# Convolution taps ahead of the steps of a block inverse, on VectorE

## The reference, cut to what matters

```python
proj = h @ mix_w_in
qkv = silu(causal_depthwise_conv(concat([q, k, v]), conv_w))      # 4 taps along the tokens
qh = l2_normalize(q) * 128 ** -0.5;  kh = l2_normalize(k);  vh = v
kk = kh @ kh^T in each chunk
a_mat = strict_lower(beta * kk * decay)
sol = triangular_solve(a_mat + I, rhs)                            # unit lower triangular
...                                                               # a scan over the chunks
```

## Time and profile before

| | us |
|---|---|
| median of 3 runs (lowest, highest) | 2188.54 (2186.83, 2190.27) |
| the profiled execution, its own time | 2190.45 |
| its span | 2188.8 |
| PE busy | 2042.5 (93%) |
| DVE busy | 1008.9 (46%) |
| ACT busy | 819.9 (37%) |
| POOL busy | 170.1 (8%) |

### The profile page before, as it was taken

The page is one execution under the profiler, slowest core; times in us unless marked ns, Lnnn a source line. Parts: engine busy times, 40 slices in busy tenths (PEclk is TensorE's granted clock), DMA queues, the critical chain, the costliest instruction groups (busy, mean ns, idle before and its releaser), DMA issues.

```text
span 2188.8 us, 26092 instructions
## 1 busy us (share of the span) xinstructions
PE 2042.5 (93%) x9478; PEld 1661.5 (76%) x9478; DVE 1008.9 (46%) x1464; ACT 819.9 (37%) x1358; POOL 170.1 (8%) x193
## 2 busy tenths in 40 slices
PE   6999876689989999999999998999989999999998
PEld 5888655566668887788888777788868877888886
DVE  6687434444434333533333375955454334333332
ACT  4342331344543233443432265433343324343332
POOL 1102002000000002000001111004300010000010
PEclk9999987589999999999999999999999999999999
DMA  8868305011103333233332322221223432333321
GB/s 286 262 177 289 108 1 118 21 41 35 39 3 99 98 99 87 77 96 96 96 99 87 114 75 71 81 71 42 58 68 89 136 97 77 97 94 102 99 86 59
DMA packets 336376, 209.63 MB, mean 96 GB/s; under 512 B 21225, under 2 KB 323238, under 8 KB 336038
## 3 DMA queue, kind: packets, MB, share of 16 engines
q1 hardware_dynamic: 325072, 170.58, 27.6%
q0 software_dynamic: 10368, 37.75, 4.9%
q10 hardware_dynamic: 854, 0.20, 0.0%
HBM read 203.26 MB, written 5.24 MB: 95 GB/s over the span
## 4 chain that ended last, share of the span: by engine, by line
PE 79%; DVE 10%; ACT 4%; DMA 3%; issue 2%; ACTq 1%; POOL 0%; DVEq 0%; SPq 0%; POOLq 0%
PE psum L425 22%; PE psum L427 21%; PE psum L426 21%; DVE delta_qkv_T L1896 2%; PE psum L1065 2%; DMA ada_w<-in_ada_w 2%; PE psum L1266 1%; PE psum L1084 1%; PE psum L1016 1%; PE psum L967 1%; PE psum L982 1%; DVE w_lo L384 1%; DVE ada_sum L1896 1%; PE psum L1074 1%; PE psum L878 1%
## 5 line engine op out<-in xcount | busy, mean ns | idle before, releaser
L425 PE MATMUL psum<-act_hi,w_hi 128*128 128x512 f32 x1616 | 649.6, 402 | 17.8 <-DVE w_lo L384 7.0
L427 PE MATMUL psum<-act_hi,w_lo 128*128 128x512 f32 x1616 | 637.0, 394 | 0.0
L426 PE MATMUL psum<-act_lo,w_hi 128*128 128x512 f32 x1616 | 636.9, 394 | 0.0
L384 DVE TENSOR_TENSOR w_lo<-w_raw,w_hi 128x1024 fp32r<-128x1024 f32 x306 | 386.1, 1266 | 376.3 <-ACT w_hi L376 354.4
L425 PEld LDWEIGHTS psum<-act_hi,w_hi 128*128 128x128 f32 x1616 | 307.7, 190 | 110.1 <-issue 42.6
L376 ACT ACTIVATE w_hi<-w_raw 128x1024 fp32r<-128x1024 f32 x306 | 319.7, 1052 | 172.2 <-PE psum L427 155.8
L427 PEld LDWEIGHTS psum<-act_hi,w_lo 128*128 128x128 f32 x1616 | 307.6, 190 | 66.5
L426 PEld LDWEIGHTS psum<-act_lo,w_hi 128*128 128x128 f32 x1616 | 308.2, 191 | 61.6 <-issue 0.5
L703 POOL TENSOR_TENSOR squares<-squares 128x512 f32<-128x512 f32 x30 | 46.2, 1549 | 1414.4 <-ACT squares L1453 911.6
L425 PE MATMUL psum<-ffn_hi,w_hi 128*128 128x512 f32 x352 | 139.6, 396 | 0.0
L427 PE MATMUL psum<-ffn_hi,w_lo 128*128 128x512 f32 x352 | 139.0, 395 | 0.0
(11 more groups left out here) (350 smaller groups left out, 2519.3 us busy)
## 6 DMA issues: line engine op xcount, KB each, us to landing
w_raw<-in_ffn_w_in SPq DMA_DIRECT2D x88, 512.0 KB, 3.8
ada_w<-in_ada_w POOLq DMA_DIRECT2D x72, 512.0 KB, 5.7
w_raw<-in_w_in SPq DMA_DIRECT2D x68, 512.0 KB, 3.9
w_raw<-in_mix_w_in SPq DMA_DIRECT2D x52, 512.0 KB, 3.8
w_raw<-in_ffn_w_out SPq DMA_DIRECT2D x32, 512.0 KB, 3.7
w_raw<-in_ffn_w_out SPq DMA_DIRECT2D x16, 384.0 KB, 3.2
w_raw<-in_w_branch_a SPq DMA_DIRECT2D x8, 512.0 KB, 3.6
w_raw<-in_w_out SPq DMA_DIRECT2D x8, 512.0 KB, 3.6
```

What stands on the lines that cost most here:

```text
L384: dve.tensor_tensor(WLO[:, n % 4, :], RAW[:, n % 4, :], WHI[:, n % 4, :].bitcast(F32), ALU.subtract).then_inc(w_lo, 1)
L425: pe.matmul(out, whi, hhi, start=start, stop=False)
L426: pe.matmul(out, whi, hlo, start=False, stop=False)
L427: return pe.matmul(out, wlo, hhi, start=False, stop=stop)
```

## The change

In the turn of the loop on DVE, `taps(t)` moves ahead of `eliminate`. `value_rows` and `inverse_less` stay ahead of both. Nothing else is changed.

```diff
@@ -2414,11 +2414,11 @@
                     chained(ts(col(QEP, 32), dcol(D_QSQ), EPS * P, EPS * EPS * P, ALU.mult, ALU.add))
                 if t >= 18:
                     value_rows(t - 18)
-                if 11 <= t < 20:
-                    eliminate(ELIMINATED[t - 11], ELIMINATED[t - 10])
                 if t == 22:
                     inverse_less(0, 0)
                 taps(t)
+                if 11 <= t < 20:
+                    eliminate(ELIMINATED[t - 11], ELIMINATED[t - 10])
             value_rows(6)
             inverse_less(0, 1)
             value_rows(7)
```

## The result

The change makes the kernel slower by about a quarter of a per cent: median 2195.0 us (20 runs, 2186.71 to 2198.62) against 2189.52 for the kernel before, run beside it (20 runs). The ratio is 1.0024, 95% interval 1.0015 to 1.0032, or +5.3 us, 3.3 to 7.0. The prediction was +4.3 us, 2192.8; the result is inside its range, and in its sign and order of size it was right.

What follows compares the result with a forecast made beforehand. The prediction took DVE to set the pace for tiles 12 to 19, TensorE afterwards. A later inverse (2.7 us) plus half clock (1.6) gave +4.3 on the 2188.54 median: 2192.8 us, range 2189.3 to 2196.3.

Steps and rivals of the forecast that it cites:

- Tile 12: At tile 12 on DVE, taps(12) wait for conv_base(12), and DVE is 1.05 us late from there.
- Tiles 13 to 17: DVE stays 1.05 us late without further waits; TensorE's waits shrink and turn(16) comes 1.54 us ahead.
- Tile 18: At turn(17), late value_rows(0) holds TensorE, which loses its lead and idles 3.07 us in one piece instead of 0.48.
- Tile 19: Elimination behind taps(19) issues the inverse's store 4.20 us late; inverse_back(0, 0), with about 1.5 to spare, shifts by 2.7.
- The clock: After tile 18's 3.07 us idling, tile 19's matmuls run at half clock, costing 1.6 us, bounds 0 and 3.4.
- The rule by which I forecast the fall: In the trace before, TensorE idling of 1.93 us and more at full clock is followed by half clock; 1.74 is not.
- The sum: Inverse's delay 2.7 plus clock 1.6 make 4.3 us, for a time of 2192.8.
- Behind 1430 ... I find nothing that gives it back: After 1430 us the chain follows TensorE through this stage, and nothing recovers the 4.3 us.
- No fall of the clock: Rival: the delay alone counts at tile 18, without half clock; +2.7 us, 2191.2, chance 0.14.
- the lead holds: Rival: DVE's lateness doesn't hold turn(17), TensorE keeps up to 2.0 us lead; -0.9 us, 2187.6, chance 0.08.
- It does nothing measurable: Rival: shorter waits at tiles 14 to 17 give back what tile 12 costs; 2188.5 us, chance 0.04.
- Two low stretches: Rival: low clock lasts 6 us and more, or a further stall; +5.7 to +6.1 us, 2194.5, chance 0.22.

Runs made afterwards that it cites:

- only12: Changed kernel edited so taps go first at tile 12 only; one execution, turn(11) to inverse_back(0, 0) +1.00 us against the kernel before.
- middle: Changed kernel edited so taps go first at tiles 13 to 17 only; +3.3 us (1.3 to 5.3) against the kernel before.
- early_old: Kernel before, elimination still first, with value_rows(t - 17) behind taps(t) replacing value_rows(t - 18) ahead of elimination; 2189.5 us, ratio 1.0005.
- change_early: Changed kernel with value_rows(t - 17) right behind taps(t), one tile earlier; 2194.95 us, ratio 1.0028 against the kernel before.
- ends: Changed kernel edited so taps go first at tiles 11, 12, 18 and 19 only; +4.2 us (2.2 to 6.1) against the kernel before.
- after: First profiled execution of the changed kernel itself, against the profile of the kernel before; 2186.71 us, span 2185.0.
- again: The changed kernel unaltered, run and profiled a second time; 2193.58 us against 2189.33 for the kernel before, ratio 1.0026.
- only19: Changed kernel edited so taps go first at tile 19 only; one execution, turn(11) to inverse_back(0, 0) +1.11 us against the kernel before.
- fill_change: Changed kernel with the first two quarters of the next stage's first tile moved ahead of turn(23); 2191.0 us, ratio 1.0009 against the kernel before.
- fill: Kernel before with the first two quarters of the next stage's first tile moved ahead of turn(23); 2188.68 us, ratio 0.9992.
- best: Kernel before with early_old's value_rows move and the two quarters ahead of turn(23); 2186.68 us, ratio 0.9983.

## Why the prediction was right, and where not

*Tile 12.* Right: 1.05 late forecast, 1.03 found, the releaser as forecast; only12 has +1.00 by that edit alone. Of the change's delay 0.83 is the idling; the other 0.2 DVE brought along from tile 11, which I had put at 0.05. The reading was incomplete: middle showed that tile 13 pays it where it is the first.

*Tiles 13 to 17.* Right: DVE neither gains nor loses, `turn(16)` 1.56 ahead (1.54 forecast), and PE's waits there, 0.63, 0.92 and 0.95 ahead of `turn(13)` to `turn(15)` before, are down to 0.33 and 0.95, ahead of `turn(15)` and `turn(16)`.

*Tile 18.* Right to the hundredth in the idling (3.07), and `turn(17)` 1.03 late. That the gate is `value_rows` and not the silu is shown by early_old, and by change_early, where the lead passes.

*Tile 19.* The store's delay without the clock was forecast as 4.20 and measured 4.21 in ends. The step that was mis-sized is the one behind it: I took 6.1 + 0.3 = 6.4 us from the store's issue to `inverse_back`, and it is 5.77 to 5.98 in the six profiles where the DMA releases it (after, again, ends, only19, change_early, fill_change). "Landed at 1427.5" was a reading of SP going on to its next DMA, not of the landing, and from the landing to the first matmul it is 0.04 us in the chain of after, not 0.3. So `inverse_back`, 7.84 us behind the store before, had about 2.0 us to spare and not 1.5: 7.84 - 5.80 = 2.04, and 4.21 - 2.04 = 2.17 instead of 2.7. The loads of w_raw behind the inverse, which I had put at nothing, did cost nothing: they come 5.3 us later in after (1427.21, before 1429.30, each from `turn(11)`), and from `turn(23)` to the end the two profiles are alike to 0.1 us.

*The clock.* The fall came as forecast, at 0.50 behind the 3.07 us, in all four profiles with that gap (after, again, middle, fill_change), and not behind the 0.48 us of ends. It cost 1.32 and not 1.6, the full change against ends (between `turn(17)` and `turn(18)` 7.30 us, where the natural 6.11 of the prediction would stand, is 1.19 of it); of the 3.4 us of half clock some 0.5 lay in the idling in the profile after. The Trainium skill, page "TensorE: Matmul & The Clock Gate", section "Why this matters for your kernels", speaks of drops from gaps in the order of 3 us; the gap of 3.07 agrees, but 1.74 was followed by a fall in six profiles of nine and 3.18 wasn't at 284.99 of the profile after, and here the measurements decide.

The rule by which I forecast the fall was wrong. I had written that in the trace of before each idling of 1.93 us and more at full clock is followed by half clock. One isn't: 2.74 us ahead of 274.62, where the clock stays at 1.00, as this row and the window behind it show:

```profile
274.62 3.30 PE L982 MATMUL psum<-mlstm_v_tokens,mlstm_decay_probs 128*128 128x257 f32 x14 [2.74 <-ACT params L1362]
274.70:281.50 6.80, 6.80 (x26) 4.77 (x26) 1.15 (x2) 1.09 (x6) 0.00 (x0) 1.00 0.01 4
```

That the 3.07 us at `turn(17)` cost the clock in four profiles of four is measured; that they had to doesn't follow from their length.

*The sum* for the stage was 4.3 and is 3.5: 2.17 + 1.32. Both terms were somewhat high. That +4.3 stands so near the measured +5.3 is in part luck: the stage came 0.8 us too high, and 1.7 us beyond the stage were missed. The range (2189.3 to 2196.3) isn't worked out from the terms either; with 1 us on either side of the two nearest rivals it would be 2190.2 to 2195.6, which the 2195.0 is still within.

*What the forecast missed.* "Behind 1430 ... I find nothing that gives it back" holds, but something is added: the time is 1.7 us (change) and 2.0 (again) beyond the stage. I had written that 1.74 us of idling are followed by no fall, from one profile of before. They often are, and profiles with the fall have 1.4 to 1.9 us more in the tail (against before's 732.7). Five kernels are 1.7 to 2.4 us beyond their stage length (change, again, ends, middle, early_old), and those without the gap only -0.8 to +0.2 (fill against its -1.02, fill_change and best against fill and the difference of their stages). This fits falls at `turn(23)` in most executions of the edited kernels and few of before, but the profiles can't show it: in the two of the change the clock held there.

The mean granted clock of every execution in the experiments is on record, though, and it points to the clock for the missing time. Its mean is 0.9561 in the 9 executions of again and 0.9580 in the 31 of before beside them. This difference of 0.0019 over 2190 us is some 8 us more at half clock (give or take 2, by the scatter of the executions), so some 4 us of time; the gap at `turn(17)` accounts for 3.4 of the 8 in the profile. Middle has 0.9563, ends 0.9570 and early_old 0.9573 against the same 0.9580. Where the further 5 us at half clock of again lie isn't recorded. It need not be `turn(23)` alone: fill, without that gap, has 0.9568 against 0.9579 in its 27 of before, and its profile the longer stretch at 1802. Which execution has which fall, and why, stays open.

*The rivals.* "No fall of the clock" and "the lead holds" are refuted, the second twice over: by the gate, and, with the gate lifted, by the inverse's landing. "It does nothing measurable" is out by the interval. "Two low stretches" has nearly the right time (+5.7 to +6.1), but not its mechanism: no profile of the change has more than 3.4 us of low clock at tile 18. Yet the mean clocks say that a typical execution does have more than one low stretch more than before; `turn(23)`, which I had excluded, is one place where profiles show another, though not those of the change.

## What to carry to other kernels

On an engine that works in order, independent work ahead of an instruction that waits is what fills its wait; before moving it back, find when the operand arrives, and expect the first moved instruction to meet the hole where the new order begins (it did at tiles 12, 13, 18 and 19 here). A lead won on one engine is worth nothing until the next thing that it needs from the late engine is earlier too, and it turns many short waits into one long one, which here cost the clock on top. To compare small edits, count from the last instruction that both share: the profile of the slower kernel had the shorter span here.

## What I had not expected of the hardware

Whether the clock falls behind a gap of 1.7 to 3.2 us isn't fixed by the gap's length: after 1.74 us of idling at the same place, in the same matmuls, it fell in six profiles and held in three; after 3.18 us at another, it fell in the profile before (288.10) and held in that after (284.99). A fall behind the 1.74 us shows as 1.4 to 1.9 us in a tail that repeats to 0.2 us in the three profiles without it. Filling that gap with work that has to be done anyway gained 1.9 us at its place in the profile of fill, and 0.9 of that went again to a longer stretch at half clock 350 us later. And the part of the program ahead of `turn(11)` took between 1361.36 and 1369.23 us in the twelve profiles, more than the whole effect of the change; the shortest has 143.4 us at half clock in it, the longest 160.4 and 163.8.
